# Softmax factors applied behind the value products, and the value products of a pair in one piece

## The reference

```
def blocked_attention(q, k, v, scale):
    def one_block(qblk):
        s = jnp.einsum('bqkgd,btkd->bkgqt', qblk, k).astype(jnp.float32) * scale
        p = jax.nn.softmax(s, axis=-1).astype(v.dtype)
        return jnp.einsum('bkgqt,btkd->bqkgd', p, v)
...
merged = jnp.concatenate([rms_norm(o_g, out_norm_gqa), rms_norm(o_m, out_norm_mla)], axis=-1)
return merged @ w_o
```

## Time and profile before

| | |
|---|---|
| Time, median of 3 runs | 2345.5 us (2342.74 to 2346.44) |
| The profiled execution's own time | 2345.05 us |
| Its span, first to last instruction | 2343.2 us |
| Mean granted TensorE clock | 0.995 |
| TensorE busy | 2280.9 us (97% of the span) |
| VectorE busy | 1360.2 us (58%) |
| ScalarE busy | 893.6 us (38%) |
| GpSimd busy | 230.8 us (10%) |

### The profile page before, as it was taken

The page is one execution under the profiler, slowest core; times in us unless marked ns, Lnnn a source line. Parts: engine busy times, 40 slices in busy tenths (PEclk is TensorE's granted clock), DMA queues, the critical chain, the costliest instruction groups (busy, mean ns, idle before and its releaser), DMA issues.

```text
span 2343.2 us, 28475 instructions
## 1 busy us (share of the span) xinstructions
PE 2280.9 (97%) x10844; PEld 1621.2 (69%) x10844; DVE 1360.2 (58%) x2231; ACT 893.6 (38%) x1550; POOL 230.8 (10%) x190
## 2 busy tenths in 40 slices
PE   8999999999999999999999999999999999999998
PEld 6754876344575478744457788888888778888886
DVE  5696654323659755433347757777435665877722
ACT  4485542111437645211133234444223233444421
POOL 2202201000230220100000011000001002000000
PEclk9999999999999999999999999999999999999999
DMA  4300439999530024899973322333333322333331
GB/s 173 99 6 23 140 149 379 410 410 410 218 101 13 19 90 180 333 409 410 410 302 124 86 90 91 99 96 94 99 99 135 112 77 90 99 99 97 101 96 49
DMA packets 112087, 381.63 MB, mean 163 GB/s; under 512 B 16464, under 2 KB 17232, under 8 KB 111696
## 3 DMA queue, kind: packets, MB, share of 16 engines
q1 hardware_dynamic: 108208, 366.80, 44.0%
q0 software_dynamic: 2304, 8.39, 0.9%
q10 hardware_dynamic: 1440, 4.62, 0.5%
HBM read 363.51 MB, written 6.29 MB: 158 GB/s over the span
## 4 chain that ended last, share of the span: by engine, by line
PE 86%; DVE 6%; DMA 3%; ACT 2%; POOL 1%; issue 1%; SPq 0%; POOLq 0%; DVEq 0%; ACTq 0%
PE ps L1346 11%; PE ps L1347 11%; PE ps L1348 11%; PE ps L1643 8%; PE ps L1370 5%; PE ps L1372 5%; PE ps L1371 5%; PE ps L1665 5%; PE ps L1532 3%; PE ps L1391 3%; PE ps L1389 3%; PE ps L1390 3%; PE ps L1482 2%; PE ps L1490 2%; DMA wa<-in_wu 1%; PE ps L1675 1%
## 5 line engine op out<-in xcount | busy, mean ns | idle before, releaser
L2463 DVE TENSOR_TENSOR wlo<-stage,whi 128x1024 fp32r<-128x1024 f32 x262 | 329.4, 1261 | 294.2 <-ACT whi L1782 293.7
L1346 PE MATMUL ps<-hTh,whi 128*128 128x512 f32 x1120 | 442.6, 395 | 0.0
L1348 PE MATMUL ps<-hTh,wlo 128*128 128x512 f32 x1120 | 437.8, 391 | 0.0
L1347 PE MATMUL ps<-hTl,whi 128*128 128x512 f32 x1120 | 437.7, 391 | 0.0
L1782 ACT ACTIVATE whi<-stage 128x1024 fp32r<-128x1024 f32 x262 | 276.0, 1057 | 328.9 <-PE ps L1372 120.6
L1346 PEld LDWEIGHTS ps<-hTh,whi 128*128 128x128 f32 x1120 | 211.2, 189 | 48.2 <-issue 4.7
L1348 PEld LDWEIGHTS ps<-hTh,wlo 128*128 128x128 f32 x1120 | 211.2, 189 | 44.6
L1347 PEld LDWEIGHTS ps<-hTl,whi 128*128 128x128 f32 x1120 | 211.2, 189 | 42.4
L2367 DVE TENSOR_TENSOR ps<-ps,Rs 128x512 f32<-128x512 f32 x124 | 86.1, 699 | 138.9 <-PE ps L1348 124.9
L2370 DVE SCALAR_TENSOR_TENSOR t<-ps,vecs,t 128x511 f32<-128x511 f32 (+1 forms) x176 | 131.1, 745 | 3.7 <-ACT t L1745 0.7
L2367 DVE TENSOR_TENSOR x<-x,ps 128x512 f32<-128x512 f32 x184 | 116.5, 682 | 28.4 <-PE ps L1372 18.0
(11 more groups left out here) (379 smaller groups left out, 4315.9 us busy)
## 6 DMA issues: line engine op xcount, KB each, us to landing
stage<-in_wpk SPq DMA_DIRECT2D x268, 512.0 KB, 3.6
wa<-in_wd SPq DMA_DIRECT2D x56, 512.0 KB, 15.3
wa<-in_wu SPq DMA_DIRECT2D x54, 512.0 KB, 15.1
wa<-in_wg SPq DMA_DIRECT2D x46, 512.0 KB, 15.4
ws<-in_wg SPq DMA_DIRECT2D x26, 512.0 KB, 13.4
ws<-in_wu SPq DMA_DIRECT2D x24, 512.0 KB, 11.9
wr<-in_wg SPq DMA_DIRECT2D x24, 512.0 KB, 15.3
stage<-in_wd SPq DMA_DIRECT2D x22, 512.0 KB, 16.4
```

Of the source, the lines that this page charges most:

```text
L1346: pe.matmul(o, h, ah, start=k == 0, stop=False)
L1347: pe.matmul(o, h, al, start=False, stop=False)
L1348: t = pe.matmul(o, lo, ah, start=False, stop=k == 7)
L2463: ve.tensor_tensor(M.wlo[i % NW][:, :], M.stage[i % NSTAGE][:, :], f(M.whi[i % NW][:, :]), ALU.subtract).then_inc(*S.wlo.mark(("w", i)))
```

## The change

The exponentials are no longer divided. Once a pair (step sums, at the second unit of the next pair) VectorE makes the reciprocal of the pair's 8 row sums, each repeated over 64 columns, into a 128 x 512 tile; TensorE turns it in four transposes behind the value products (step shares), which gives the factors in the layout of the output; ScalarE copies the undivided output, and VectorE multiplies it in place. The turns follow the scores by two steps instead of three, and VectorE copies two turned tiles of four. The value products of all four key blocks of a pair come in one piece, behind the scores of the fourth unit of the next pair.

```
-LAG = 5
+LAG = 4
-DVE_TURN = 1
+DVE_TURN = (1, 3)
...
             if kt == KT - 1:
-                self.do("att_out", kind, l, p, ub[p])
+                b = self.take()
+                self.do("shares", l, p, b)
+                self.do("att_out", kind, l, p, ub[p], b)
                 self.drop(ub[p])
-                if kind == "mix":
-                    self.att_sums(l, p)
+                self.drop(b)
+                self.att_sums(l, p)
...
-                plan.setdefault(per * (i + 1) - 1 + LAG + (step * kt if i < npair - 1 else kt), []).append((p, kt))
+                plan.setdefault(per * (i + 1) - 1 + LAG, []).append((p, kt))
         for i in range(max(plan) + 1):
             if i < nu:
                 scores(i)
                 between(i)
-            elif i - 2 < nu:
-                self.do("share", kind, l, i - 2)
+            if i > per and i % per == 1:
+                self.do("sums", l, i // per - 1)
             self.tick()
             for p, kt in plan.get(i, []):
                 values(p, kt)
-            if 0 <= i - 3 < nu:
-                turn_p(i - 3)
+            if 0 <= i - 2 < nu:
+                turn_p(i - 2)
```

On TensorE:

```
-            q.wait_ge(*S.dve.at("share", kind, l, n))
+            q.wait_ge(*S.act.at("exp", kind, l, n))
...
-                    q.wait_ge(*S.act.at("PT", kind, l, NT * g + 3))
-                    q.wait_ge(*S.dve.at("PT", kind, l, NT * g + DVE_TURN))
+                    q.wait_ge(*S.act.at("PT", kind, l, NT * g + 2))
+                    q.wait_ge(*S.dve.at("PT", kind, l, NT * g + 3))
...
+        elif name == "shares":
+            l, p, u = a
+            o = claim(u)
+            q.wait_ge(*S.dve.at("sums", l, POS["mix"][p]))
+            r = M.tmp[4 + POS["mix"][p] % 2]
+            for m in range(NT):
+                t = pe.transpose(o[:, m * 128:(m + 1) * 128], r[:, m * 128:(m + 1) * 128], M.ident)
+            t.then_inc(*S.pe.mark(("shares", l, p)))
```

On ScalarE, in att_out:

```
+            copy(M.oT[:, POS["mix"][p], :], M.ps[u[0]][:, :], ("oU", l, p), ("free",) + u)
+            if p == 7:
+                q.wait_ge(*S.dve.at("oT", l, p))
+                q.wait_ge(*S.pool.at("osq_add", l, OSQ_PAST[p]))
+                copy(M.osq[OSQ[p]][:, :], M.oT[:, POS["mix"][p], :], ("osq", l, p), f=ACT.Square)
```

On VectorE the calls of total and share in the step scores go, with both functions, and these are added:

```
+        elif name == "sums":
+            l, i = a
+            q.wait_ge(*S.act.at("exp", "mix", l, 8 * i + 7))
+            if i > 1:
+                q.wait_ge(*S.pe.at("shares", l, SEQ["mix"][i - 2]))
+            c = 65 + 16 * (i % 2)
+            s = M.st[:, c:c + 15:2].rearrange("p (h m) -> p m h", h=2)
+            ve.reciprocal(M.tmp[4 + i % 2][:, :].rearrange("p (m h f) -> p m h f", m=NT, h=2),
+                          s.unsqueeze(3).to_broadcast([128, NT, 2, 64])).then_inc(*S.dve.mark(("sums", l, i)))
         elif name == "att_out":
-            kind, l, p, u = a
+            kind, l, p, u, *b = a
+            if kind == "mix":
+                q.wait_ge(*S.act.at("oU", l, p))
+                q.wait_ge(*S.pe.at("shares", l, p))
+                o = M.oT[:, POS["mix"][p], :]
+                tt(o, o, M.ps[b[0][0]][:, :], ALU.mult, ("oT", l, p), ("free",) + b[0])
```

More of the change, by code:

```diff
@@ L318, in spread, with attention @@
         self.later.append(rows)
-    def attention(self, kind, l, npair, nhead, nk, step, between):
+    def attention(self, kind, l, npair, nhead, nk, between):
         KT = nk // 128
@@ L504, in mixer @@
         halves = {42: 0, 46: 1, 50: 0, 54: 1}
-        self.attention("mix", l, 8, 2, 512, 2, between)
+        self.attention("mix", l, 8, 2, 512, between)
         self.do("point", "attended", l)
@@ L1864, in act_program @@
             i, r = divmod(n, NHEAD[kind] * NT)
-            c = 64 + 4 * (n % 8)
+            c = 64 + 2 * (n % 16)
+            if n > 15:
+                q.wait_ge(*S.dve.at("sums", l, n // 8 - 2))
             q.wait_ge(*S.dve.at("ng", kind, l, n))
@@ L1872, in act_program @@
             copy(M.Pr[kind][n % 4][:, :], M.ps[u[0]][:, 0:nk], ("exp", kind, l, n), ("free",) + u, f=ACT.Exp,
-                 bias=M.st[:, c:c + 1], accum_out=M.st[:, c + 2:c + 3])
+                 bias=M.st[:, c:c + 1], accum_out=M.st[:, c + 1:c + 2])
         elif name == "turn_p":
@@ L1877, in act_program @@
             PT = M.PT[kind]
-            if n % 4 == DVE_TURN:
+            if n % 4 in DVE_TURN:
                 continue
@@ L1908, in act_program @@
         elif name == "att_out":
-            kind, l, p, u = a
-            q.wait_ge(*S.pe.at("values", kind, l, p))
+            kind, l, p, u, *_ = a
             if kind == "mem":
+                q.wait_ge(*S.pe.at("values", kind, l, p))
                 q.wait_ge(*S.pe.at("point", "memory", l))
@@ L2163, in pool_program @@
         elif name == "att_out":
-            kind, l, p, u = a
+            kind, l, p, u, *_ = a
             if kind == "mem" or p == 7:
                 continue
-            q.wait_ge(*S.act.at("oT", l, p))
+            q.wait_ge(*S.dve.at("oT", l, p))
             q.wait_ge(*S.dve.at("heads", l, ("q1", "q2")[OSQ[p] // 2]))
@@ L2385, in signed_sines @@
         after_own()
[L2387 to L2396, removed]
     def mshare(l, d):
@@ L2599, in dve_program @@
             kind, l, n, u = a
-            c = 64 + 4 * (n % 8)
-            if n > 1:
-                total(kind, l, n - 2)
+            c = 64 + 2 * (n % 16)
             q.wait_ge(*S.pe.at("scores", kind, l, n))
-            if n > 7:
-                q.wait_ge(*S.dve.at("share", kind, l, n - 8))
+            if n > 15:
+                q.wait_ge(*S.act.at("exp", kind, l, n - 16))
             ve.tensor_reduce(M.st[:, c:c + 1], M.ps[u[0]][:, 0:NKEY[kind]], AX.X, ALU.max, negate=True).then_inc(
                 *S.dve.mark(("ng", kind, l, n)))
-            if n > 1:
-                share(kind, l, n - 2)
         elif name == "turn_p":
             kind, l, n, u = a
-            if n % 4 != DVE_TURN:
+            if n % 4 not in DVE_TURN:
                 continue
@@ L2636, in dve_program @@
             mshare(*a)
-        elif name == "share":
-            total(*a)
-            share(*a)
-        elif name == "att_out":
-            kind, l, p, u = a
+        elif name == "sums":
[7 more added lines that the diff above has]
+                          s.unsqueeze(3).to_broadcast([128, NT, 2, 64])).then_inc(*S.dve.mark(("sums", l, i)))
+        elif name == "att_out":
+            kind, l, p, u, *b = a
[4 more added lines that the diff above has]
+                tt(o, o, M.ps[b[0][0]][:, :], ALU.mult, ("oT", l, p), ("free",) + b[0])
             if kind == "mem":
@@ L2663, in dve_program @@
                 q.wait_ge(*(S.dve if g else S.pool).at("lo", ("y", l), i - 2))
-            q.wait_ge(*S.act.at("oT", l, i))
+            q.wait_ge(*S.dve.at("oT", l, i))
             keys = [("y", l, g, j)]
```

## The result

The changed kernel takes 2385.7 us (median of 4 runs, 2384.3 to 2387.0) beside 2345.7 us before (four runs; the table above has three of them): ratio 1.0173, 95% interval 1.0155 to 1.0190. It is slower by 40 us, as forecast in kind and within the range; the size forecast was 50.

A forecast was written before the change was run, and what follows sets the result against it. TensorE, busy 97% of the span, was taken to bound the kernel. A layer: -1.2 + 13.2 + 3.6 + 2.3 = +17.9 us, two +36, clock +14: +50 on 2345.05 gives 2395 us, range 2355 to 2430.

The forecast's parts named there:

- The mechanism and its place: In VectorE's queue the long reciprocal precedes a key copy that the value products need; TensorE stands about 3 us.
- The reciprocal's price: The new 512-element reciprocal on VectorE, once a pair, takes 4.1 us, at 7.7 ns an element; ends 0.68 and 4.4.
- the slope is 6 and the time 3.2 us: Alternative reciprocal price if short forms ran back to back and gained 10 ns; takes 15 us off the forecast.
- The clock: 16 TensorE waits of 2.2 to 3.6 us may drop the granted clock; 0.9 us each, +14 us.
- Grouped-query pairs: Attention pairs of this kind take 15.8 us against 12.5 before; four pairs add 13.2 us a layer.
- Two more waits of 0.1 us: Within a grouped-query pair, after the turns of a+12, TensorE waits only this much more before scores a+17.
- Latent pairs: The two full latent windows take 37.2 us together instead of 33.6: +3.6 us a layer.
- one output scaling: In the latent pairs, a 128x512 VectorE operation now ahead of a key copy, costing 0.8 us.
- Start and tail: Each attention stage's first turns come earlier, -1.2 us; its last stretch and closing chain take +2.3 us.
- Rival 1: The reciprocal is long, but the clock stays up: 2381 us, chance 0.17.
- Rival 2: The reciprocal is an ordinary 0.7 us operation and TensorE never waits for the key copy: 2327 us, chance 0.16.
- slower beyond about 1.9 us: Reciprocal length above which the change turns slower; above 0.7 us each microsecond costs 16 to 17 us.

The follow-up runs named there:

- A: Changed kernel with the reciprocal made of the 8 row sums alone (128x8), then spread to 128x512 by a VectorE copy: 2344.5 us, ratio 0.9998.
- B: Changed kernel with its long reciprocal two units later, behind the last key copy: 2358.1 us, ratio 1.0054.
- C: Changed kernel with the 128x512 reciprocal made twice into the same tile: 2472.4 us, ratio 1.0551.
- H: Changed kernel with eight small matmuls behind the first value product of each pair: 2385.2 us, ratio 1.0176.
- I: Changed kernel, long reciprocal kept, with turns three steps behind the scores and products 5 behind: 2381.6 us, ratio 1.0159.
- e1_small: The kernel of A: changed kernel with a 128x8 reciprocal and a spread copy: 2344.5 us, ratio 0.9998.
- D: Kernel before with reciprocals of 1 to 512 elements, one with repeated input, and a repeating copy added at the very end: 2352.9 us.
- e12_long3: The kernel of I: changed kernel with turns three steps behind the scores and products 5 behind: 2381.6 us, ratio 1.0159.

## Why the prediction was right, and where it was off

- **The mechanism and its place: right.** "The reciprocal stands in front of the value products": the idle time of TensorE there ended with VectorE's key copy, and A, B and C show it by taking the length away, moving the place and doubling it.
- **The reciprocal's price: too high.** Taken 4.1 us, measured 3.35. The slope of 7.7 ns an element came from a row of 155 ns, made up of instructions right behind others on VectorE; with waits between them, 1 element took 163 ns, and the measured slope is 6.25. The prediction had named this ("the slope is 6 and the time 3.2 us") and not taken it. The term is 0.75 x 16 = 12 us too high.
- **The clock: right in kind, half the size.** Forecast 14 us as 0.9 for each of 16 waits; measured about 7 (H), in 4 of them. The waits of the grouped-query pairs, forecast at about 3.4 us, cost 2.6 us, as they should with a reciprocal of 3.35; in the profile's count they are 1.68 us, and the clock stayed up behind all eight. Which waits drop it the forecast couldn't say, and the runs don't settle it either (I).
- **Grouped-query pairs: too low for their reciprocal.** With 3.35 us the forecast's sum gives 15.0 us a pair; they took 15.4 to 17.1. The step that failed is "Two more waits of 0.1 us": the turns waited 1.4 us a pair, as in A. In one pair a layer VectorE's query split took 1.80 us instead of 0.69 beside an addition of GpSimd:

```profile
164.99 1.29 POOL L2188 TENSOR_TENSOR sq<-sq,raw 128x512 f32<-128x512 f32 x1
165.02 1.80 DVE L2382 SCALAR_TENSOR_TENSOR qs<-raw,qs 64x512 fp32r<-64x512 f32 x1
...
168.39 0.63 PE L1493 MATMUL ps<-c,Pr 128*128 128x128 f32 x4 [1.34 <-ACT Pr L1756]
```

  The turns behind it waited 1.34 us, and that unit took 2.44 us where the others of its kind took 1.32. With the short distance such a delay passes straight on to TensorE.
- **Latent pairs: "one output scaling" ahead of a key copy was too little.** Forecast 37.2 us for the two (35.7 with the right reciprocal), measured 38.9 in layer 0, of which 1.4 is the clock. In the second of them VectorE makes two scalings around the reciprocal, the first of them at 1.44 us twice as long as an ordinary operation of that size:

```profile
205.37 1.44 DVE L2382 SCALAR_TENSOR_TENSOR tmp<-oT,vecs,raw 128x512 f32<-128x512 f32 x1
...
210.59 0.65 DVE L2382 SCALAR_TENSOR_TENSOR tmp<-oT,vecs,raw 128x512 f32<-128x512 f32 x1
211.16 0.68 DVE L2621 COPY PT<-ps 128x512 f32<-128x512 f32 x1
```

  The products there waited 3.15 us, in the latent pair before 1.08. That is 2.1 us more, where the forecast had 0.8.
- **Start and tail: right.** The first pair took 11.9 us, after 12.6 and 13.3; forecast -1.2. From scores 57 to the output projection TensorE took 27.0 us in layer 0 instead of 25.0; the forecast was +2.3, from which its two reciprocals, each 0.75 us too long, would take 1.5, and the clock's fall behind the last wait adds 1.5.
- **The sum.** 36 - 12 + 7 = 31 us by the forecast's own steps with measured prices; the stages grew by 41.5. The missing 10 us go by pairs, in layer 0, to the grouped-query pairs (4.6 us) and the two latent pairs (1.8), less what the last stretch came out shorter. So two errors, too high by 19 us and too low by 10, cancelled in part: that the time came out only 10 us below the forecast is in part luck. Rival 1's 2381 us, with a clock that stays up, is nearer still, but the clock did fall (H).
- **Rival 2** priced the kernel with an ordinary reciprocal at 2327 us; e1_small, which is nearly that kernel (0.2 + 0.43 us for 0.7), took 2344.5. Here too the turns' waits were left out: the grouped-query pairs took 12.8 to 14.4 us where the rival has 12.2, the two latent pairs 33.8 where it has 31.0. Its turning point, "slower beyond about 1.9 us", was therefore too high: already at 0.65 us nothing is gained.

What stays open: what makes the clock fall behind one wait and not behind an equal one, and whether GpSimd's addition is the cause of the split of 1.80 us; no kernel took it away.

## What to carry to other kernels

Making one long instruction out of many short ones saves busy time and can still lose, if the long one stands in an in-order queue ahead of something that the bounding engine needs: ask for the longest instruction ahead of each hand-over, not for the sum. Take the reciprocal (or any slow operation) of the few distinct numbers and spread the result with a copy: 0.2 + 0.43 us instead of 3.35. Joining the bounding engine's work into long pieces pays only if the others can catch up between the pieces; check their pace per unit there, and leave a step more of distance. Look at the end of the stage apart from its middle: most of what joining gained here was gained there.

## What the runs showed of the hardware

- A reciprocal on VectorE takes 6.25 ns an element and partition in fp32 (D), against about 1 ns for the plain operations of the earlier trace rows; the step from 1 to 2 elements (163 and 166 ns) doesn't show it.
- The length of a wait alone doesn't say whether the granted clock falls behind it. Behind a wait of 2.02 us it fell to 1.2 GHz in layer 1 of the kernel before and not in layer 0; behind one of 3.65 us it fell in layer 1 of e12_long3 and behind one of 3.66 us in its layer 0 it didn't. It fell behind all four waits of 2.37 and 3.15 us of the changed kernel and all 16 of 4.65 us and more (C), and behind none of those of 1.68 us. A fall cost 1.4 to 2.9 us of products.
- A VectorE operation of 64x512 from and to SBUF took 1.80 us instead of 0.69 while GpSimd had an addition of 1.29 us under way, once in each layer of the changed kernel.
